# Recurrence preparation moved from two stages of its own into the convolved projection, on one Trainium2 core

## The reference, cut to what matters

```python
mod = cs @ ada_w[l] + ada_b[l]                       # both layers, 6 * 1024 columns each
h = rmsnorm(x, norm_g[l, 0]) * (1.0 + sc1) + sh1
z = h @ mix_in[e]                                    # 1024 x 1024 by 1024 x 3584
za = dwconv3(z[..., :2048], mix_conv[e])             # three taps over the tokens
r, k, v, u = jnp.split(za, 4, -1)                    # 512 wide each
g = jax.nn.sigmoid(uf @ g1) @ g2
kk = hs(kf * k_k)
kk = kk * lax.rsqrt(jnp.sum(kk * kk, -1, keepdims=True) + L2_EPS)
for d in range(2):
    w_log = -jax.nn.softplus(-(w0[d] + jnp.tanh(uf @ w1[d]) @ w2[d])) - 0.5
    a = jax.nn.sigmoid(a0[d] + (uf @ a1[d]) @ a2[d])
    kd = hs(kf * (1.0 + (a - 1.0) * k_a))
    y = y + wkv7_scan(rh, hs(decay), kd, vh, kk, hs(a), reverse=(d == 1))
    bonus = bonus + jnp.sum(rh * kd * r_k, -1, keepdims=True) * vh
```

## Time and profile before

| | |
|---|---|
| runs | 3069.54, 3072.76, 3077.79 us; median 3072.76 |
| profiled execution | 3071.72 us, of which its span is 3069.9 us |
| busy in the span | PE 2658.7 us (87%), DVE 1577.3 (51%), ACT 1129.5 (37%), POOL 979.2 (32%) |
| TensorE clock granted | mean 0.931 of full speed |

### The profile page before, as it was taken

One profiled execution on the slowest core, in us unless ns is written; L12 is line 12 of the kernel. 1 busy time (PEld: TensorE's weight loads), 2 busy tenths in 40 slices (PEclk: granted clock), 3 DMA queues, 4 the chain that ended last, 5 costly groups with the idle time before them and its releaser, 6 DMA issues. The chain is left out here.

```text
span 3069.9 us, 55055 instructions
## 1 busy us (share of the span) xinstructions
PE 2658.7 (87%) x23104; PEld 2154.1 (70%) x23104; DVE 1577.3 (51%) x2253; ACT 1129.5 (37%) x1774; POOL 979.2 (32%) x660
## 2 busy tenths in 40 slices
PE   2698997965789989558899999999778899999998
PEld 1576775731789889347688888877556688888887
DVE  4463664503555454416555556445626555556445
ACT  2211224523434333224344444445324344444434
POOL 0411111003212111142577775000131577775000
PEclk9799998987899999769899999999879899999999
DMA  4555745046311310332222223754032222223654
GB/s 167 161 179 175 240 171 149 16 148 245 93 44 47 83 44 4 117 118 83 70 84 85 85 83 131 245 170 148 30 96 83 75 88 85 83 83 135 236 187 143
DMA packets 301852, 361.14 MB, mean 118 GB/s; under 512 B 31652, under 2 KB 227585, under 8 KB 301613
## 3 DMA queue, kind: packets, MB, share of 16 engines
q1 hardware_dynamic: 291966, 351.38, 35.1%
q10 hardware_dynamic: 9648, 6.34, 0.6%
HBM read 282.12 MB, written 75.55 MB: 117 GB/s over the span
## 5 line engine op out<-in xcount | busy, mean ns | idle before, releaser
L2401 POOL TENSOR_TENSOR cg_u_lo<-cg_u_raw,cg_u_hi 128x512 fp32r<-128x512 f32 x216 | 329.3, 1533 | 136.4 <-ACT cg_u_hi L2287 136.4
L304 PE MATMUL cg_ps<-m_hi,cg_u_hi 128*128 128x512 f32 x844 | 331.3, 393 | 33.0 <-POOL cg_u_lo L2401 28.7
L306 PE MATMUL cg_ps<-m_hi,cg_u_lo 128*128 128x512 f32 x844 | 330.8, 392 | 0.0
L305 PE MATMUL cg_ps<-m_lo,cg_u_hi 128*128 128x512 f32 x808 | 316.0, 391 | 0.0
L2287 ACT ACTIVATE cg_u_hi<-cg_u_raw 128x512 fp32r<-128x512 f32 x216 | 132.1, 629 | 386.5 <-PE cg_ps L306 234.1
L304 PEld LDWEIGHTS cg_ps<-m_hi,cg_u_hi 128*128 128x128 f32 x844 | 159.9, 189 | 68.2 <-POOL cg_u_lo L2401 29.5
L304 PE MATMUL cg_ps<-over_y_tx,cg_u_hi 128*128 128x512 f32 x480 | 186.7, 389 | 0.0
L305 PE MATMUL cg_ps<-over_y_tx,cg_u_hi 128*128 128x512 f32 x480 | 186.7, 389 | 0.0
L306 PE MATMUL cg_ps<-over_y_tx,cg_u_lo 128*128 128x512 f32 x480 | 186.7, 389 | 0.0
L306 PEld LDWEIGHTS cg_ps<-m_hi,cg_u_lo 128*128 128x128 f32 x844 | 159.7, 189 | 33.6
L2451 DVE SCALAR_TENSOR_TENSOR cg_z<-cg_ps,top_conv_f,cg_z 128x1023 f32<-128x1023 f32 x88 | 112.9, 1283 | 133.8 <-ACT cg_z L2311 133.8
(11 more groups left out here) (416 smaller groups left out, 6691.8 us busy)
## 6 DMA issues: line engine op xcount, KB each, us to landing
cg_u_raw<-in_ffn_up SPq DMA_DIRECT2D x88, 512.0 KB, 5.3
cg_u_raw<-in_ffn_down SPq DMA_DIRECT2D x64, 512.0 KB
za_mw<-in_ada_w SPq DMA_DIRECT2D x12, 2048.0 KB
over_f_d_raw<-in_ffn_down SPq DMA_DIRECT2D x48, 512.0 KB
scr_act<-cg_z SPq DMA_DIRECT2D x44, 512.0 KB, 2.7
qkv_mw<-in_ada_w SPq DMA_DIRECT2D x8, 2048.0 KB
mod_w<-in_ada_w SPq DMA_DIRECT2D x8, 1024.0 KB
za_w_raw<-in_mix_in SPq DMA_DIRECT2D x16, 512.0 KB, 4.3
```

Source lines behind the costliest of these rows:

```text
L304: nc.tensor.matmul(out, a_hi, b_hi, start=first, stop=False)
L305: nc.tensor.matmul(out, a_hi, b_lo, start=False, stop=False)
L306: return nc.tensor.matmul(out, a_lo, b_hi, start=False, stop=last)
L2401: G.tensor_tensor(u_lo[:, n % RING], source(g, i), u_hi[:, n % RING].bitcast(F32), ALU.subtract).then_inc(ulo_done, 1)
```

## The change

`lora_hidden`, `prepare_recurrence` and their two blocks are gone. `project_and_prepare` replaces `project_convolved`: the tiles now come in the order u, k, then r and v in turn, and stay in SBUF; between the tiles TensorE makes the hidden layers (`L`), decays, rates and gate (`N`), squares (`S`), spread roots (`X`) and bonus (`H`), into two PSUM results `pr` that are used in turn. The list `ORDER` names them in their order. The loop is written out, the weight buffers are two instead of four, and u is not stored. Eight chunks of layer 1 (`M0` to `M7`) are made beside the first eight tiles, with their weights in the buffers of later results (`out`, r and v). The other four chunks of layer 1 move to `project_qkv`, which now makes twelve.

```diff
-        CM = 6 * D // CHUNK - HEAD
+        CE = 6 * D // CHUNK
+        CM = CE - HEAD + 4
         def summed_at(c):
-            return 4 + 3 * c if c < 5 else 18 + 2 * (c - 5)
+            return 3 + 2 * c if c < 7 else 17 + 3 * (c - 7) // 2
...
+    TILES = [3 * KU + f for f in range(KU)] + [KU + f for f in range(KU)] + [t for f in range(KU) for t in (f, 2 * KU + f)]
+    ORDER = ("M0 M1 M2 L0 M3 L1 M4 M5 L2 M6 M7 N00 N01 S0 S1 N02 N03 N04 S2 S3 N10 N11 N12 N13 N14 H0 X0 X1 N20 N21 X2 N22 N23 N24 H1 X3 "
+             "N30 N31 N32 N33 N34 H2 H3").split()
...
+        ps, pr = s.ps("ps", [P, 2, S]), s.ps("pr", [P, 2, S])
...
+            load(0)
+            load(1)
+            load_chunk(0)
+            load_chunk(1)
...
+            load(2)
+            for c in range(2, MC):
+                load(c + 1)
+                load_chunk(c)
...
+            store_z(8, r_stored[0])
+            load(13)
+            for i in range(4):
+                store_out(1, i)
+            store_z(9, v_stored[0])
+            store_vr(0)
+            load(14)
...
+            store_z(15, v_stored[1])
+            store_vr(3)
+            store_bon(3)
...
+            def free(name):
+                n = ORDER.index(name)
+                if n >= 2:
+                    read(pe, ORDER[n - 2])
...
+            def both_ways(f, i, net, hid):
+                names = f"N{f}{i}", f"N{f}{i + 1}"
+                for name in names:
+                    free(name)
+                cols = slice(f * P, (f + 1) * P)
+                for half in range(2):
+                    span = slice(half * HALF, (half + 1) * HALF)
+                    for d in range(2):
+                        rows = slice(d * 64, (d + 1) * 64)
+                        ins = mm(result(names[d])[:, span], net[rows, cols], hid[rows, span], start=True, stop=True)
+                        if half:
+                            ins.then_inc(small_mm, 1)
...
+            tile(7)
+            chunk_sum(6)
+            chunk_sum(7)
+            decays(0)
+            squares(0)
+            squares(1)
+            tile(8)
+            rates(0)
+            gated(0)
+            squares(2)
+            squares(3)
+            tile(9)
+            decays(1)
+            rates(1)
+            tile(10)
+            gated(1)
+            bonus(0)
+            roots(0)
+            roots(1)
+            tile(11)
+            decays(2)
+            roots(2)
+            tile(12)
+            rates(2)
+            gated(2)
+            bonus(1)
+            roots(3)
+            tile(13)
+            decays(3)
+            tile(14)
+            rates(3)
+            gated(3)
+            bonus(2)
+            tile(15)
+            bonus(3)
...
+            def step(p):
+                middle(p)
+                if p + 2 < M:
+                    split(p + 2)
...
+            A(root[:, :], root[:, :], ACT.Sqrt, bias=eps[:, 0:1]).then_inc(root_in, 1)
+            rate(0)
+            step(9)
+            sigmoids(1, 0, W0)
+            sigmoids(1, 2, A0)
+            reverse(0)
+            step(10)
...
+            for p in range(11):
+                low(p)
+            sum_rates(0)
+            times_key(0)
+            low(11)
+            sum_rates(1)
+            low(12)
+            times_key(1)
+            low(13)
+            low(14)
...
+            for c in range(MC):
+                chunk_rows(c)
+                convolve(c)
...
+            convolve(15)
+            bonus(3)
...
-                lora_hidden(nc, scr["z"], a["rwkv_w1"], a["rwkv_a1"], a["rwkv_g1"], tw, ta, tg)
-                prepare_recurrence(nc, scr["z"], a["rwkv_w2"], a["rwkv_a2"], a["rwkv_g2"], tab, consts, tw, ta, tg, scr["lw"], scr["aa"],
-                                   scr["kk"], scr["bon"], scr["gate"], scr["vr"])
```

More of the change, by code:

```diff
@@ new lines, in project_and_prepare @@
+        tw, ta, tg, gate, vr, bon, root = (s.sb(n, [P, S]) for n in ("tw", "ta", "tg", "gate", "vr", "bon", "root"))
+        out = s.sb("out", [P, 4, S])
+        pick, spread = s.sb("pick", [P, 32]), s.sb("spread", [P, P])
+        rest, eps = s.sb("rest", [P, KU]), s.sb("eps", [P, 1])
+        ps, pr = s.ps("ps", [P, 2, S]), s.ps("pr", [P, 2, S])
+        raw_loaded = [s.sem(f"raw_loaded{j}") for j in range(2)]
+        r_stored, v_stored = ([s.sem(f"{n}{j}") for j in range(2)] for n in ("r_stored", "v_stored"))
@@ new lines, in squares, with sigmoids @@
+            def squares(f):
+                multiplied(act, f"S{f}")
+                rows = slice(32 * f, 32 * f + 32)
+                A(root[rows, :], result(f"S{f}")[rows, :], ACT.Copy).then_inc(act_read, 1)
+            def sigmoids(f, i, vec_at):
+                for d in range(2):
+                    name = f"N{f}{i + d}"
+                    multiplied(act, name)
+                    if f:
+                        act.wait_ge(out_stored[i + d], 16 * f)
+                        if i == 2:
+                            act.wait_ge(asum, f)
+                    A(out[:, i + d, :], result(name), ACT.Sigmoid, bias=vec[:, vec_at + d, f:f + 1]).then_inc(act_read, 1)
@@ new lines, in _ @@
+            split(0)
+            split(1)
+            for p in range(3):
+                step(p)
+            chunk_out(0)
+            step(3)
+            chunk_out(1)
+            step(4)
+            chunk_out(2)
+            hidden(0, tw, ACT.Tanh)
+            step(5)
+            chunk_out(3)
+            hidden(1, ta, ACT.Copy)
+            chunk_out(4)
+            step(6)
+            chunk_out(5)
+            hidden(2, tg, ACT.Sigmoid)
+            key(0)
+            key(1)
+            step(7)
@@ new lines, in bonus @@
+            def bonus(f):
+                multiplied(dve, f"H{f}")
+                dve.wait_ge(conv_done, at(V, f) + 1)
+                if f:
+                    dve.wait_ge(bon_stored, 16 * f)
+                else:
+                    for j in range(2):
+                        dve.wait_ge(m_stored[j], 16 * MC // 2)
+                X.tensor_tensor(bon[:, :], result(f"H{f}"), vt[:, f % 2, :], ALU.mult).then_inc(dve_read, 1)
+            X.tensor_scalar(rest[:, :], vec[:, K_A, :], -2.0, 2.0, ALU.mult, ALU.add).then_inc(rest_set, 1)
```

717 lines of the change are left out of this document (377 added, 340 removed).

## The result

The changed kernel takes 3033.78 us (median of 4 runs, 3029.97 to 3035.47), the kernel before 3073.94 us in the runs beside it. The ratio is 0.9868, with a 95% interval of 0.9851 to 0.9885. The forecast was 3036, with a range of 3012 to 3058. In a later comparison the same kernel took 3032.89 us (median of 4 runs), ratio 0.9875 (0.9859 to 0.9891).

The account below looks back on a forecast made before the run. TensorE bounds the projection; the low-rank stages mostly wait. Removed stretch -123.6, products +65.5, switching +2, waits +13.0, sums -3.4 +3.4 +1.0, stall +3.6, tail +1.8 gave -36.7: 3035.0 profiled, median 3036 us, range 3012 to 3058.

Parts of the forecast that it names:

- The stretch removed: From the first DMA of `lora_hidden` to the first of `recurrence`, between barriers: removing it takes off 123.6 us whole.
- Small products and switching, +67.5: In the projection, TensorE pays small products in full, 65.5 us, plus 2 for changing between kinds of products.
- rival B: In the projection's groups, the halves of a pair don't overlap: +14.4 us, total 3050; chance 0.09.
- Waits, +13.0: Behind projection tiles 7 to 14, TensorE waits for ScalarE to read the two result buffers: 13.0 us together.
- Rival A: Waits in the projection and `project_qkv` are mostly absorbed because ScalarE reads sooner: -13.0 and -3.6 us, total 3020; chance 0.16.
- The clock: TensorE's clock was expected at 1.00 through the lengthened projection, so no cost was counted for it there.
- a fall in the groups: Sign against the forecast: TensorE's clock dropping in the small-product groups between the projection's tiles.
- Rival C: The clock falls in the projection's five groups with waits of 1.7 to 4.0 us: +14.5 if all, total 3050; chance 0.15.
- Chunk sums and the stall in the qkv stage, +8.0: In `project_qkv`: more sums +3.4 us, the twelfth behind the last tile +1.0, longer wait for chunk 4's load +3.6.
- Chunk sums out of the projection, -3.4: The projection has eight chunk sums instead of eleven before its last tile, at 1.14 us each: -3.4 us.
- The tail, +1.8: After the projection's last taps: the bonus product on VectorE and two more DMA issues on SyncE, +1.8 us.
- Weights late (rival D): Weight loads for projection tiles 11 to 15 stuck behind stores on SyncE: some 8 us each, total 3076; chance 0.05.

Follow-up runs that it names:

- experiment 4: Changed kernel with each of three hidden-layer products using one of four row blocks of u; projection stage 249.7 us, 14.9 less.
- experiment 5: Changed kernel with both products of each decay or rate pair on rows 0 to 63, so they can't overlap; projection stage 277.9 us, 13.4 more.
- the second profile: Changed kernel profiled again without any edit; projection stage 269.0 us against 264.6 in its first profile.
- the third profile: Changed kernel profiled once more without any edit, beside later versions; projection stage 263.7 us, median of its runs 3032.89 us.
- the early load: Changed kernel with the load of qkv's chunk 4 ahead of the last four raw-weight loads on SyncE's queue; qkv stage 161.7 us, 5.8 less.

## Why the prediction was right

The sum was -36.7 us against its profiled execution and -42.0 were found. The mechanism held: a stretch between barriers was removed whole, and its products came back as TensorE's own work and as waits for ScalarE. That the total is so near is in part luck, since some 11 us were counted too many and 5 to 6 left out. Step by step:

- **The stretch removed**: exact. It lay between barriers, so its length was its price.
- **Small products and switching, +67.5**: in the trace the groups between the tiles (with `bonus(3)`) take 84.6 us; less the waits of 11.7, less eight chunk sums of 0.95, less 1.8 of a pair at half clock, 63.4 are left. That products are paid one for one is shown for the hidden layers by experiment 4, the overlap of pairs by experiment 5; rival B is dead. The excess of 4 is the squares (2.84 and 3.02 us for two, where 3.8 was counted) and the 2 us for switching, of which nearly nothing is seen.
- **Waits, +13.0**: 11.7, and at the places named: behind tile 7 1.84 + 1.23 (3.3), behind 8 1.24 (1.7), behind 9 3.76 (4.0), behind 10 0 (0), behind 11 and 12 1.24 each (1.7), behind 13 0 (0), behind 14 1.20 (0.6). Rival A is dead: the readings stand behind the tile's own work in ScalarE's order, and 1.24 us is what a third product waits behind a pair.
- **The clock**, taken at 1.00: this is the term that was missing, though it cost little. Two falls cost 1.8 in the pair, 0.5 in tile 10 and 1.4 in tile 11, 3.7 us; in the second profile the pair and tiles 10 to 12 cost about 7. The prediction named a fall in the groups as a sign that it was wrong, and that sign came. Rival C, with its chance of 0.15, was half the truth: it had the fall only behind waits and at every one. Here the waits of up to 1.84 us behind tiles 7 and 8 left the clock at 1.00 (401 to 441 us), the one of 3.76 did not in seven of eight profiles, nor did one of 2.04 in experiment 5. Ahead of the fall in tile 11 there was no wait for 22 us. The Trainium skill ("TensorE: Matmul & The Clock Gate", section "A second HAM failure mode: psum-queue depth-cycling") speaks of short gaps between groups of matmuls that make the clock swing; the trace agrees for the long wait, not for the short ones behind tiles 7 and 8.
- **Chunk sums and the stall in the qkv stage, +8.0**: +5.4. The mechanism is shown: chunk 4's rows began at 185.19 (185.7 forecast), held by the DMA. TensorE waited 7.24 us, not 8.5, so the stall grew by 2.3 and not 3.6; but the wait at this place went from 7.12 to 9.39 us over the profiles of kernels with the same code there, so the 8.5 was as good as one profile can tell. The twelfth sum at the end cost nothing, not 1.0: from the last product's end to the next stage's first transfer it is 3.96 us in both kernels (272.94 to 276.90, before 267.24 to 271.20).
- **Chunk sums out of the projection, -3.4**: a sum takes 0.95 us there, not the 1.14 of the qkv stage, so three fewer are -2.9. The tiles themselves, without the two falls, were 0.9 longer together, 0.4 of it in the first, which begins at half clock.
- **The tail, +1.8**: +1.5, near the forecast. Its stores go out at 552.86, 553.94 and 554.31, and the next stage begins 5.66 us behind the last of them; before it was 3.66 behind the one.
- **Weights late (rival D)**: no wait at `za_ps` other than the stage's first. Dead.
- The remaining 2.6 us, attention and recurrence, are within what such stages differ by between two profiles.

So the forecast counted 4.1 us too many for products, 1.3 for waits, 2.6 in the qkv stage and 0.3 in the tail, and attention and recurrence came out 2.6 shorter: 10.9. It left out 3.7 of the clock, 1.4 in the projection's sums and tiles and 0.4 at the starts of the stages: 5.5. The difference is the 5.3 us, to rounding.

## What to carry to other kernels

A stage between barriers was moved here into one that TensorE bounds, and the price of its matmuls could be read off before (67.5 forecast, 63.4 found). What remained were waits for the engine that reads the results, and counting through that engine's order gave each of them within 0.6 us. Look there first for a table load or a second result that a product need not wait for: moving one pair by a tile was worth 2.8 us by order alone, and moving one DMA issue ahead of four others some 6 to 9 in the qkv stage. Where a stage's length differs by 5 us between two profiles of the same kernel, read its clock windows before explaining any edit by it, and its first tile too: that alone differed by up to 1.5 us between profiles.

## What the runs showed of the hardware

- TensorE's granted clock fell to half in the middle of unbroken work, right behind products that use 32 of 128 rows (469 to 473 us: 0.57 with PE busy 4.00 of 4.00), and in other profiles inside such a product that stood behind a wait of 1.24 us (482 to 483 us of the third profile: 0.57). One or both were seen in 8 of 9 profiles, and with the same products on 128 rows in none of 3. A fall cost 1.4 to 2.9 us in tile 11 or 12. That the rows are the cause is likely and not shown.
- The clock was half behind waits of 3.76 us in seven of eight profiles and behind one of 2.04 us in the one profile that has it; waits of 1.23 to 1.84 us behind tiles 7 and 8 left it at 1.00.
- Two products with 32 result rows at different quarters of the result (the squares, 128 rows in) overlapped in part: 2.91 us for two, where one took 1.90. Two with 32 rows in and 128 out (the roots), on different quarters of the rows, took 3.37 to 3.78 us for two, where one took 1.98. Two with 64 rows in, one on each half of the rows, took 1.99 for two, and 3.67 on the same half.
- The same seven sums by rows on VectorE took 5.48 us, and 8.22 with the early load (177 to 185 us), where GpSimd was making low parts of weights until 181.6; what slowed them was not tested.
